# Dense feed-forward of a hybrid decoder step: what the first down-projection unit waits for, and which PSUM banks the down outputs use

## What the kernel computes

```python
for l in range(2):
    h = h + mixer(rmsnorm(h, norm_mix[l]))        # HGRN2 heads and Mamba-2 heads side by side
    hn = rmsnorm(h, norm_ffn[l])
    if l == 0:                                    # dense SwiGLU, inner width 2816
        g, u = split(hn @ w_ffn_in, 2)
        h = h + (silu(g) * u) @ w_ffn_out
    else:                                         # top-2 of 8 experts, inner width 3584
        h = h + moe(hn)
y = rmsnorm(h, norm_final)
```

## Time and profile before

| what | us |
|---|---|
| time, median of 3 runs (lowest, highest) | 1978.37 (1975.26, 1980.34) |
| the profiled execution's own time | 1978.76 |
| its span, first to last instruction | 1977.0 |
| PE busy in the span | 1854.8 (94%) |
| DVE busy | 1346.6 (68%) |
| ACT busy | 1046.3 (53%) |

### The profile page before, as it was taken

How to read it: one execution, slowest core, us unless ns; L and a number is a source line. 1 busy time by engine, 2 the same in 40 slices (tenths; PEclk the granted TensorE clock), 3 DMA queues, 4 the chain that set the end, 5 groups by cost and what they waited for, 6 DMA issues and landing times.

```text
span 1977.0 us, 25921 instructions
## 1 busy us (share of the span) xinstructions
PE 1854.8 (94%) x9997; PEld 1609.8 (81%) x9997; DVE 1346.6 (68%) x1177; ACT 1046.3 (53%) x913; POOL 76.0 (4%) x85
## 2 busy tenths in 40 slices
PE   6998988998989989977999999999999999999995
PEld 5987877998979978765888888888888888888884
DVE  3636544444346355545988889889898898888986
ACT  3443223333233333223677767776777767677674
POOL 2002120000000021300000000000000000000000
PEclk9998869999989979787999999999999999999997
DMA  7432143443452521142999999999999999999992
GB/s 238 149 109 57 35 115 104 150 150 110 124 173 89 168 51 35 42 160 69 340 361 331 351 339 346 363 328 355 363 321 355 333 353 363 322 357 342 344 352 98
DMA packets 267757, 452.11 MB, mean 229 GB/s; under 512 B 41242, under 2 KB 102930, under 8 KB 267688
## 3 DMA queue, kind: packets, MB, share of 16 engines
q1 hardware_dynamic: 265824, 447.51, 65.6%
q0 software_dynamic: 1600, 3.46, 0.8%
q10 hardware_dynamic: 264, 0.17, 0.1%
HBM read 440.14 MB, written 10.97 MB: 228 GB/s over the span
## 4 chain that ended last, share of the span: by engine, by line
PE 89%; DVE 7%; ACT 2%; issue 1%; DMA 0%; POOL 0%; DVEq 0%; SPq 0%; ACTq 0%
PE ps L1473 16%; PE ps L1474 16%; PE ps L1999 10%; PE ps L1468 7%; PE ps L1469 7%; PE ps L2014 5%; PE ps L1547 3%; PE ps L1913 3%; PE ps L1654 2%; PE ps L1639 2%; DVE cvt L1018 1%; PE ps L1928 1%; PE ps L2042 1%; PE ps L1809 1%; DVE spL L916 1%
## 5 line engine op out<-in xcount | busy, mean ns | idle before, releaser
L1364 DVE TENSOR_TENSOR spL<-ring,spH 128x2048 fp32r<-128x2048 f32 x339 | 771.8, 2291 | 115.7 <-ACT spH L847 115.6
L847 ACT ACTIVATE spH<-ring 128x2048 fp32r<-128x2048 f32 x339 | 648.5, 1916 | 134.2 <-PE ps L2014 72.8
L1473 PE MATMUL ps<-spH,XH 128*128 128x512 f32 x896 | 357.6, 399 | 1.5 <-DVE XL L1376 1.5
L1474 PE MATMUL ps<-spH,XL 128*128 128x512 f32 x896 | 352.3, 393 | 0.0
L916 DVE TENSOR_TENSOR spL<-ring,spH 128x2048 fp32r<-128x2048 f32 (+1 forms) x74 | 158.3, 2146 | 236.8 <-ACT spH L572 236.7
L1468 PE MATMUL ps<-hnH,spH 128*128 128x320 f32 x928 | 276.0, 312 | 13.7 <-DVE hnL L934 7.1
L1469 PE MATMUL ps<-hnL,spH 128*128 128x320 f32 x928 | 274.4, 310 | 0.0
L572 ACT ACTIVATE spH<-ring 128x2048 fp32r<-128x2048 f32 (+1 forms) x74 | 132.7, 1798 | 246.0 <-PE ps L1547 108.3
L1999 PE MATMUL ps<-spL,XH 128*128 128x512 f32 x896 | 242.4, 392 | 0.0
L1473 PEld LDWEIGHTS ps<-spH,XH 128*128 128x128 f32 x896 | 169.0, 189 | 38.4 <-issue 1.7
L1999 PEld LDWEIGHTS ps<-spL,XH 128*128 128x128 f32 x896 | 168.8, 188 | 37.4
(11 more groups left out here) (321 smaller groups left out, 2118.7 us busy)
## 6 DMA issues: line engine op xcount, KB each, us to landing
ring<-in_w_exp_in_dram SPq DMA_DIRECT2D x227, 1024.0 KB, 7.3
ring<-in_w_exp_out_dram SPq DMA_DIRECT2D x112, 1024.0 KB, 7.1
ring<-in_w_in_dram SPq DMA_DIRECT2D x28, 1024.0 KB, 5.9
ring<-in_w_ffn_in_dram SPq DMA_DIRECT2D x22, 1024.0 KB, 5.2
ring<-in_w_ffn_out_dram SPq DMA_DIRECT2D x16, 704.0 KB, 4.6
ring<-in_w_out_dram SPq DMA_DIRECT2D x8, 1024.0 KB, 5.2
out_dram<-ring SPq DMA_DIRECT2D x32, 256.0 KB, 2.6
ring<-in_state_hgrn_dram SPq DMA_DIRECT2D x16, 256.0 KB, 3.8
```

The lines of the kernel that those rows point to most:

```text
L847: A(esplit(j)[0], src, ACT.Copy).then_inc(S("hi_done"), 1)
L1364: V.tensor_tensor(lo, eslot(j)[0], hi.bitcast(F32), ALU.subtract).then_inc(S("split_done"), 1)
L1473: mm(out, x[0], w, start=start, stop=False)
L1474: return mm(out, x[1], w, start=False, stop=False)
```

## The change

The first unit of output 0 no longer waits for all 11 pairs of `hfL`. It waits for 10, and its second unit waits for 11. Output m goes to PSUM bank (m + 4) mod 8 in place of bank m, so outputs 0 to 3 lie in banks 4 to 7 and outputs 4 to 7 in banks 0 to 3; DVE reads them from there. Nothing else differs, and the order of the outputs stays.

```diff
-                        V.tensor_tensor(xT[:, m], xT[:, m], ps[:, m, 0:TOK], ALU.add).then_inc(S("down_evac"), 1)
+                        V.tensor_tensor(xT[:, m], xT[:, m], ps[:, (m + 4) % 8, 0:TOK], ALU.add).then_inc(S("down_evac"), 1)
...
-                    pe.wait_ge(S("hfL_done"), 11)
                     for m_ in range(8):
+                        bank = (m_ + 4) % 8
                         for half in range(2):
                             u = PLAN["down", 0] + 2 * m_ + half
+                            if m_ == 0:
+
+                                pe.wait_ge(S("hfL_done"), 10 if half == 0 else 11)
                             pe.wait_ge(S("hi_done"), u + 1)
                             wH, wL = unit(u, 11)
                             for k in range(11):
                                 kk = 11 * half + k
-                                high(ps[:, m_, 0:TOK], wH[:, k], (hfH[:, kk], hfL[:, kk]), start=kk == 0)
+                                high(ps[:, bank, 0:TOK], wH[:, k], (hfH[:, kk], hfL[:, kk]), start=kk == 0)
                             pe.wait_ge(S("split_done"), u + 1)
                             for k in range(11):
                                 kk = 11 * half + k
-                                m = mm(ps[:, m_, 0:TOK], wL[:, k], hfH[:, kk], start=False, stop=kk == 21)
+                                m = mm(ps[:, bank, 0:TOK], wL[:, k], hfH[:, kk], start=False, stop=kk == 21)
                             m.then_inc(S("used"), 1)
```

## The result

| | before | changed |
|---|---|---|
| median of 9 runs each, us | 1977.38 | 1967.81 |
| lowest to highest | 1972.78 to 1980.34 | 1954.68 to 1971.79 |
| profiled execution, own time | 1978.76 | 1971.79 |
| its span | 1977.0 | 1970.0 |

The ratio is 0.9943 with a 95% interval of 0.9921 to 0.9966: faster, by 6.7 to 15.6 us.

The account below looks back on a forecast made before the run. PE, busy 94%, was taken as the bound, idling 5.5 us before the first down unit and then starting slowly. Idle 4.7 plus slow steps 2.5 gave -7.2 us, other terms 0: median 1971.2 us, range 1968 to 1975.5.

Parts of the forecast that it names:

- What the first unit needs; PE goes straight on: First down unit: pairs, bank and weights ready by 484.46, so PE starts it at about 488.2 without waiting.
- The gain is 501.36 - 494.13 = 7.2: Second down unit: its second matmul starts at 494.13 instead of 501.36, 7.2 us earlier.
- Its two parts, 4.7 and 2.5: Start of down projection: idle time falls from 5.5 to 0.9 us (4.7), about 21 slow steps vanish (2.5).
- The clock stays up: Pause before the second down unit: 0.86 us brings no slow stretch, as a 1.45 us pause kept clock 1.00; no loss.
- Rival A: Second down unit: the clock falls all the same, costing 2.5 us; time 1973.7, chance 0.09.
- The third unit's cover: Third down unit: ACT's split and the low part (497.3) finish before PE wants them at 498.8; cover 1.5 us, cost 0.
- It reaches the end: After the down phase: its end moves from 574 to 567, and norm, mixer, router and experts end 7 us earlier.
- Rivals B and D: Gain swallowed later by the experts' weight stream, or something else held the first unit; time 1978.4, chance 0.09 together.
- rival C: Layer 1: starting 7 us earlier meets the clock's control badly and runs slower; 1984.4 us or more, chance 0.04.
- The signs of being wrong: First down unit after 488.5, clock 0.50 after 493.9, third unit waiting for ACT, or post-down stretch over 2 us longer.
- 2 us for the median of few runs: Whole-kernel time: range allowance of 2 us, the three runs of before spreading over 5 us.
- 2 us for luck in layer 1: Layer 1's mixer: range allowance of 2 us either way, from identical matmuls taking 180.8 and 182.8 us.

Follow-up runs that it names:

- e3: Kernel before plus 36 matmuls into free bank 7 in PE's idle time ahead of the first down unit; 1976.14 us, ratio 1.0003.
- e5: Changed kernel plus 49 matmuls (7.2 us of PE work) ahead of the last down unit; 1976.11 us, ratio 0.9996 to the kernel before.
- e7: Kernel before plus 24 matmuls in PE's idle time ahead of the first down unit, leaving a 2.03 us pause; one run, 1980.98 us.
- e2: Changed kernel with its new banks, but the first down unit waits for all 11 pairs again; 1977.48 us, ratio 1.0007 to the kernel before.
- e1: Changed kernel run again without edit, 12 runs; 1969.54 us against 1977.06 for the kernel before, ratio 0.9967.
- e4: Changed kernel with the wait for pair 11 moved to the second down unit's block 20, which first reads it; 1968.32 us, ratio 0.9964 to before.
- e6: Changed kernel a third time, without edit, 6 runs; 1967.89 us, ratio 0.9955 to the kernel before.
- e8: Kernel before plus 12 matmuls in PE's idle time ahead of the first down unit, leaving a 3.79 us pause; one run, 1983.85 us.

## Why the prediction was right in its steps and wrong in its range

- *What the first unit needs; PE goes straight on.* Right: no pause at 491.27.
- *The second unit waits for the same instruction.* Right, and its size too. The trace's idle time of 0.71 us starts at the modelled end of the last matmul. From start to start, as the working counted, PE asks at 495.97 + 0.15 = 496.12 (the last of the 11 low products starts at 494.50 + 1.78 - 0.31) and starts at 496.99: 0.87 us, where 0.86 were worked out.
- *The gain is 501.36 - 494.13 = 7.2.* Right: 7.18, 7.19 and 7.17 us in the three profiles of the changed kernel (90.03, 90.02 and 90.04 against 97.21).
- *Its two parts, 4.7 and 2.5.* 4.8 and 2.3 (e3). The working took 5.5 us from a modelled end and 0.86 from start to start; on one count it is 5.54 - 0.71 or 5.70 - 0.87, both 4.83.
- *The clock stays up.* Right: the windows show 1.00 in all three profiles of the changed kernel and in e5, and in e7 after 2.03 us of pause. Rival A is out for this place. The pause stands between the two units of output 0, which share bank 4, so nothing here tests many small pauses with a new bank after each.
- *PE beside ACT and DVE costs nothing.* Right: the chain from ACT's split to PE's start took 493.91 - 488.47 = 5.44 us with PE idle and 496.99 - 491.53 = 5.46 with PE at work.
- *The third unit's cover.* The moments are right (all 3.1 us later here): ACT's split ends at 497.38 + 1.38 = 498.76, DVE's low part at 498.80 + 1.63 = 500.43, and PE starts the unit at 501.94 without a wait. The cover of 1.5 us is the low part's against the unit's start, but PE reads the low part only after the unit's 22 high products. The cover of what it needs first is 3.2 us.
- *Banks.* Right: 0 between the landmarks (97.26 against 97.21, e2).
- *It reaches the end.* Nothing is swallowed in the experts: from their first matmul (L1971, L1974 in the changed kernel) to the start of their last ones behind DVE's L1424 (L1979, L1982) the changed kernel took 1947.48 - 910.63 = 1036.85 us, the kernel before 1954.45 - 917.29 = 1037.16. Rivals B and D are out, and so is rival C, by the sign.
- *The signs of being wrong.* By the letter one came: PE starts its first down unit at 491.27, after 488.5. But the whole execution lies 3.1 us later there, and against ACT's split of the second unit PE starts 0.26 us ahead, where 488.47 - 488.2 = 0.27 was forecast. The other three did not come. The stretch from the end of the down phase to the end of the span did not grow, it shrank by 2.9 us (1403.0 to 1400.1).

The step that failed is in "How the numbers follow": the term *2 us for the median of few runs*, read off the 5 us between three runs. The mechanism was right, and this term of the range was mis-sized. The forecast median, 1971.2, and the measured one, 1967.81, lie 3.4 us apart. Of this, 1.0 us is the base: the first three runs of before have the median 1978.37, the nine beside the changed kernel 1977.38. The other 2.4 us are the changed kernel's.

What the runs showed in its place: over all sets the kernel before ran 61 times, from 1963.28 to 1983.87 us with a standard deviation of 4.2, and the changed one 27 times, from 1954.68 to 1973.81, with 4.1. Drawn at random from these, the median of three runs of before scatters with a standard deviation of 2.5 us and the median of nine of the changed kernel with 1.0. The difference of the two then spans 6.5 us with 1 in 10 left out at either end. So the term should have been about 3.2 us and not 2. With the 2 us for layer 1 combined as the prediction did it (the root of the sum of squares), the range would have begun at 1967.4 and held the result.

Of the first 9 runs of the changed kernel two were far below the rest, at 1954.68 and 1957.94 with mean clock 0.958 and 0.956, where the others had 0.947 to 0.951; the kernel before has such runs too, 3 of 61 below 1965. That nine runs held two of them is luck: the other 18 runs of the changed kernel begin at 1962.55.

The second allowance, *2 us for luck in layer 1*, left out that the parts ahead of the change vary as well. The table gives, for every profile, the first landmark, the distance, the time from the second landmark to the first expert matmul, and the experts, in us:

| profile | first landmark | distance | layer 1 up to the experts | experts |
|---|---|---|---|---|
| before | 488.47 | 97.21 | 331.61 | 1037.16 |
| changed | 491.53 | 90.03 | 329.07 | 1036.85 |
| e1, changed again | 487.19 | 90.02 | 330.19 | 1037.01 |
| e2, banks alone | 488.82 | 97.26 | 328.83 | 1036.87 |
| e3, 36 matmuls | 489.38 | 94.88 | 330.90 | 1037.02 |
| e4, late pair | 488.00 | 89.05 | 329.62 | 1037.03 |
| e5, shifted back | 487.64 | 97.23 | 329.80 | 1037.01 |
| e6, changed again | 487.76 | 90.04 | 330.16 | 1037.07 |
| e7, 24 matmuls | 490.68 | 94.87 | 334.07 | 1037.06 |
| e8, 12 matmuls | 493.56 | 97.20 | 331.62 | 1037.15 |

The first landmark lies ahead of anything that the change touches and varies by 6.4 us; layer 1 varies by 5.2, the experts by 0.3, and the distance by 0.06 at most for the same work. In the profiled pair the changed kernel came 3.06 us later to the first landmark, gained 7.18 by the change, and was 2.54 us shorter in layer 1 and 0.31 in the experts. That sums to the 7.0 us, and only the 7.18 are shown to be the change's.

The long and the short stretches differ in the mean clock. Two windows with the same 1749 matmuls of layer 0, of the changed kernel's first profile and of e1's (their edges lie partly in idle time of PE; from the mixer's first matmul to the first up matmul it is 302.2 and 297.9 us):

```profile
31.50:334.00 302.50, 275.48 (x1749) 251.39 (x1749) 152.94 (x219) 103.06 (x158) 31.17 (x28) 0.88 0.34 101
```

```profile
31.50:329.00 297.50, 268.39 (x1749) 246.41 (x1747) 152.74 (x216) 102.34 (x158) 31.25 (x28) 0.90 0.35 103
```

The same 1842 matmuls of layer 1 took 330.2 us at 0.88 in e1 and 334.1 at 0.86 in e7:

```profile
577.20:907.40 330.20, 288.97 (x1842) 260.14 (x1843) 164.07 (x268) 111.10 (x171) 31.30 (x28) 0.88 0.28 82
```

```profile
585.50:919.60 334.10, 293.35 (x1842) 264.16 (x1843) 164.04 (x268) 111.26 (x171) 31.17 (x28) 0.86 0.27 81
```

Over whole runs it is the same. In the 52 runs of before whose mean clock is on record, time and clock go together (correlation -0.91, about 1.6 us less for each 0.001 more), and in the 27 of the changed kernel too (-0.91, 1.4 us).

What stays open: all 27 runs of the changed kernel against all 61 of before give medians 8.7 us apart (95% interval 6.9 to 10.3, by resampling). That holds 7.2, but its middle is 1.5 us more. A fit of the time to the mean clock and the kernel puts the changed kernel 5.2 us lower at equal mean clock (standard error 0.5), which is near the idle part of 4.8. So the 1.5 us seem to lie in a higher mean clock, beyond what the slow start gives back; this is argued from a fit, not shown by a trace. Whether the changed kernel meets the clock in layer 1 a little more kindly on average, or the two lowest runs account for it, the runs don't settle. Without those two the changed kernel's mean is 1968.7, which is 7.7 us below the mean of before, 1976.4; but the kernel before keeps its own lowest runs in that comparison.

## What to carry to other kernels

A wait put ahead of a loop often asks for all that the loop will read; ask what its first iteration reads, and where it writes, and let the outputs go to the buffers that come free first. A pause of TensorE costs more than its length if the granted clock falls behind it: here 5.5 us of pause cost 7.9 us in all, counted as idle time and slow start. When a gain is a few us in a program whose other parts vary by as much from run to run, measure it in the profile between two landmarks that enclose the edit, and take the width of the forecast's range from many runs, not from three. Nor is one profile of each kernel enough for the whole time: here the pair agreed with the forecast only because two differences elsewhere nearly cancelled.

## What the runs showed of the hardware that was not expected

One execution differs from the next by nearly as much as the change's local effect: 6.4 us at a point that all kernels reach by the same instructions. Nearly all of it seen here is in the two mixers, stretches with pauses, where the mean granted clock was 0.86 to 0.90 in the windows read (layer 0's mixer took 297.8 to 304.3 us in the ten profiles, its first matmul came at 30.98 to 32.48, and the up projection varied by 1.3 us); the expert phase, with its clock at 0.99, repeats to 0.3 us in 1037.

A pause of 2.03 us left the clock at 1.00 and one of 3.79 us was followed by 0.50. After 3.79 us the slow start cost as much as after 5.54 us: the distances are 97.20 and 97.21 us.
